# Softmax and memory heads: the value product of a block issued two steps behind its transpose instead of one, with three buffers for the split block

## What is computed

```python
sc = jnp.einsum('bhqd,bhkd->bhqk', q_blk, k).astype(jnp.float32) * scale
sc = jnp.where(key_pos <= q_pos, sc, -jnp.inf)
p = jax.nn.softmax(sc, axis=-1)
return jnp.einsum('bhqk,bhkd->bhqd', p.astype(v.dtype), v)
```

## Time and profile before

| | |
|---|---|
| median of 3 runs | 3078.08 us (3076.92 to 3081.86) |
| span of the profiled execution | 3078.6 us |
| its own time apart from the span | not recorded; the span stands for it |
| mean granted TensorE clock | 0.939 of 2.4 GHz |
| latent heads, five loop passes and the closing one | 1840 to 2261 us of the span |
| memory heads' attention | 113 to 157 us and 1567 to 1611 us |

### The profile page before, as it was taken

The page is one execution under the profiler, slowest core; times in us unless marked ns, Lnnn a source line. Parts: engine busy times, 40 slices in busy tenths (PEclk is TensorE's granted clock), DMA queues, the critical chain, the costliest instruction groups (busy, mean ns, idle before and its releaser), DMA issues. The chain is left out here.

```text
span 3078.6 us, 40579 instructions
## 1 busy us (share of the span) xinstructions
PE 2705.0 (88%) x13104; PEld 2209.8 (72%) x13104; DVE 1480.0 (48%) x2547; ACT 1295.7 (42%) x2794; POOL 1038.7 (34%) x722
## 2 busy tenths in 40 slices
PE   5679999878999998998668668888879899998999
PEld 4567777657788887887548657777757688887887
DVE  5636666744755553111562236666643755553111
ACT  4436566634333332222442246666633433332222
POOL 2035555530544443443102011111120544443443
PEclk9899999989999999999788879999989999999999
DMA  3021000041222223454102000000041222223454
GB/s 111 11 65 28 28 27 27 7 171 69 82 82 82 82 82 144 143 171 147 39 14 57 23 12 18 19 18 18 9 169 69 82 82 82 82 82 134 143 171 140
DMA packets 143097, 232.38 MB, mean 75 GB/s; under 512 B 17056, under 2 KB 93856, under 8 KB 143008
## 3 DMA queue, kind: packets, MB, share of 16 engines
q1 hardware_dynamic: 143008, 231.24, 22.7%
HBM read 182.98 MB, written 48.23 MB: 75 GB/s over the span
## 5 line engine op out<-in xcount | busy, mean ns | idle before, releaser
L1487 POOL TENSOR_TENSOR l0s_run_lo<-l0s_run,l0s_run_hi 128x512 fp32r<-128x512 f32 (+3 forms) x144 | 177.2, 1231 | 200.9 <-DVE l0s_run_hi L1653 200.9
L365 POOL TENSOR_TENSOR l0f_dn_lo<-l0f_dn_raw,l0f_dn_hi 128x1024 fp32r<-128x1024 f32 x44 | 106.0, 2411 | 138.9 <-ACT l0f_dn_hi L431 138.9
L365 POOL TENSOR_TENSOR l1f_dn_lo<-l1f_dn_raw,l1f_dn_hi 128x1024 fp32r<-128x1024 f32 x44 | 106.0, 2412 | 138.3 <-ACT l1f_dn_hi L431 138.3
L82 PE MATMUL banks<-l0f_dn_hi,l0f_a_hi 128*128 128x512 f32 x352 | 139.4, 396 | 8.9 <-issue 5.3
L82 PE MATMUL banks<-l1f_dn_hi,l1f_a_hi 128*128 128x512 f32 x352 | 138.6, 394 | 9.5 <-issue 5.3
L82 PE MATMUL banks<-l1f_T_hi,l1f_op_hi 128*128 128x512 f32 x352 | 139.3, 396 | 7.4 <-DVE l1f_T_lo L538 7.2
L82 PE MATMUL banks<-l0f_T_hi,l0f_op_hi 128*128 128x512 f32 x352 | 140.1, 398 | 6.1 <-DVE l0f_T_lo L538 5.9
L84 PE MATMUL banks<-l0f_T_hi,l0f_op_lo 128*128 128x512 f32 x352 | 139.0, 395 | 0.0
L83 PE MATMUL banks<-l0f_dn_lo,l0f_a_hi 128*128 128x512 f32 x352 | 138.9, 395 | 0.0
L84 PE MATMUL banks<-l0f_dn_hi,l0f_a_lo 128*128 128x512 f32 x352 | 138.8, 394 | 0.0
L84 PE MATMUL banks<-l1f_T_hi,l1f_op_lo 128*128 128x512 f32 x352 | 138.8, 394 | 0.0
(11 more groups left out here) (480 smaller groups left out, 8572.1 us busy)
## 6 DMA issues: line engine op xcount, KB each, us to landing
l0f_raw<-in_w_ffn_gu_dram SPq DMA_DIRECT2D x22, 1024.0 KB, 5.2
l0f_dn_raw<-in_w_ffn_down_dram SPq DMA_DIRECT2D x44, 512.0 KB, 3.9
l1f_raw<-in_w_ffn_gu_dram SPq DMA_DIRECT2D x22, 1024.0 KB, 5.1
l1f_dn_raw<-in_w_ffn_down_dram SPq DMA_DIRECT2D x44, 512.0 KB, 3.9
hidden_rows<-l0f_hid SPq DMA_DIRECT2D x22, 512.0 KB, 2.7
l0f_a_raw<-hidden_rows SPq DMA_DIRECT2D x44, 256.0 KB, 3.1
hidden_rows<-l1f_hid SPq DMA_DIRECT2D x22, 512.0 KB, 2.7
l1f_a_raw<-hidden_rows SPq DMA_DIRECT2D x44, 256.0 KB, 3.0
```

The costliest lines, as they stand in the source:

```text
L82: pe.matmul(out, l_hi, r_hi, start=first, stop=False, skip_group_check=True)
L365: pool.tensor_tensor(dn_lo[e][:], dn_raw[e][:], as_f32(dn_hi[e][:]), ALU.subtract).then_inc(dn_lo_done, 1)
L1487: pool.tensor_tensor(run_lo[t % NR][:, f:HALF], run[t % NR][:, f:HALF], as_f32(run_hi[t % NR][:, f:HALF]), ALU.subtract).then_inc(run_spli ...
```

## The change

V is issued behind T(tau) for block tau-2 instead of tau-1 (`LAG`), and `pt_hi` and `pt_lo` have three buffers instead of two (`NP`); there are still two PSUM banks for the transposes. The end of a job, E, moves with V by one step. "values 0", which overwrites the values of head 0, moves from tau 13 to 14, since V(11) still reads them. The third buffer needs room: some small tiles move between two memory areas, and `k_rope` is placed where the latent heads' tiles may overlap it.

```diff
+    NP = 3
+    LAG = 2
...
-        self.pt_hi = [mem(f"{tag}_pt_hi{s}", [P, HALF], F32R) for s in range(2)]
-        self.pt_lo = [mem(f"{tag}_pt_lo{s}", [P, HALF], F32R) for s in range(2)]
-        self.nmx, self.rsum, self.rinv = (mem(f"{tag}_{n}", [P, 4]) for n in ("nmx", "rsum", "rinv"))
+        self.pt_hi = [mem(f"{tag}_pt_hi{s}", [P, HALF], F32R) for s in range(self.NP)]
+        self.pt_lo = [(low_mem if s == 2 else mem)(f"{tag}_pt_lo{s}", [P, HALF], F32R) for s in range(self.NP)]
+        self.nmx, self.rsum, self.rinv = (low_mem(f"{tag}_{n}", [P, 4]) for n in ("nmx", "rsum", "rinv"))
...
-                if tau:
-                    steps.append(("V",) + self.of(tau - 1))
-                    if j == 0:
+                if tau >= self.LAG:
+                    steps.append(("V",) + self.of(tau - self.LAG))
+                    if n and j == self.LAG - 1:
                         steps.append(("E", n - 1))
...
-        steps += [("V",) + self.of(self.nt - 1), ("E", self.nj - 1)]
+        steps += [("V",) + self.of(tau) for tau in range(self.nt - self.LAG, self.nt)]
+        steps.append(("E", self.nj - 1))
...
-                act.wait_ge(self.pv_made, 1 + turn * self.nt + max(tau - 1, 0))
-                act.activation(self.pt_hi[tau % 2][:, c0:HALF], self.t_ps[tau % 2][:, c0:HALF],
+                act.wait_ge(self.pv_made, 1 + turn * self.nt + max(tau - self.NP + 1, 0))
+                act.activation(self.pt_hi[tau % self.NP][:, c0:HALF], self.t_ps[tau % 2][:, c0:HALF],
...
-              10: ["rotate 1", "turn 0"], 11: ["used 1", "turn 1"], 12: ["turn 2"], 13: ["values 0", "turn 3"],
-              14: ["turn 4"], 16: ["turn 5"], 18: ["turn 6"], 21: ["turn 7"]}
+              10: ["rotate 1", "turn 0"], 11: ["used 1", "turn 1"], 12: ["turn 2"], 13: ["turn 3"],
+              14: ["values 0", "turn 4"], 16: ["turn 5"], 18: ["turn 6"], 21: ["turn 7"]}
```

More of the change, by code:

```diff
@@ L771, with __init__ @@
 class Attend:
-    def __init__(self, nc, ctx, tag, mem, psum, k, jobs, keys_of, blocks_of, causal, scores, values, store,
+    NP = 3
+    LAG = 2
+    def __init__(self, nc, ctx, tag, mem, low_mem, psum, k, jobs, keys_of, blocks_of, causal, scores, values, store,
                  rows_mem, ring, score_banks, out_banks=(6, 7), plan=None, extras={}):
@@ L893, in pe @@
                     pe.wait_ge(self.out_done, 1 + turn * self.nj + max(n + 1 - len(self.o_ps), 0))
-                pe.matmul(o[:, c0:HALF], self.values(h, j), self.pt_hi[tau % 2][:, c0:HALF],
+                pe.matmul(o[:, c0:HALF], self.values(h, j), self.pt_hi[tau % self.NP][:, c0:HALF],
                           start=j == 0, stop=False, skip_group_check=True)
-                pe.matmul(o[:, c0:HALF], self.values(h, j), self.pt_lo[tau % 2][:, c0:HALF], start=False,
+                pe.matmul(o[:, c0:HALF], self.values(h, j), self.pt_lo[tau % self.NP][:, c0:HALF], start=False,
                           stop=tau + 1 == self.first[n + 1], skip_group_check=True).then_inc(self.pv_made, 1)
@@ L950, in dve @@
                 dve.wait_ge(self.hi_done, turn * self.nt + tau + 1)
-                dve.tensor_tensor(self.pt_lo[tau % 2][:, c0:HALF], self.t_ps[tau % 2][:, c0:HALF],
-                                  as_f32(self.pt_hi[tau % 2][:, c0:HALF]), ALU.subtract).then_inc(self.split_done, 1)
+                dve.tensor_tensor(self.pt_lo[tau % self.NP][:, c0:HALF], self.t_ps[tau % 2][:, c0:HALF],
+                                  as_f32(self.pt_hi[tau % self.NP][:, c0:HALF]), ALU.subtract).then_inc(self.split_done, 1)
             elif kind == "E":
@@ L1330, in memory_heads @@
         jobs = [(h, half) for h in range(MEM_HEADS) for half in range(2)]
-        at = Attend(nc, ctx, f"{tag}a", mem, psum, k, jobs, lambda tile: MEM, lambda half: MEM // P, False, scores,
+        at = Attend(nc, ctx, f"{tag}a", mem, mem, psum, k, jobs, lambda tile: MEM, lambda half: MEM // P, False, scores,
                     lambda h, j: v[:, j, h, :],
@@ L2067, in scores @@
             return pe.matmul(out[:, rows], k["ident_r"][:], k["causal"][:], start=False, stop=True, skip_group_check=True)
-        at_ = Attend(nc, ctx, f"{tag}a", low, psum, k, [(h, half) for h in range(2) for half in range(2)],
+        at_ = Attend(nc, ctx, f"{tag}a", low, mem, psum, k, [(h, half) for h in range(2) for half in range(2)],
                      lambda tile: (tile + 1) * P, lambda half: 4 * half + 4, True, scores,
@@ L2360, in build @@
                 ckv = {h: mem(f"ckv_{h}", [P, KV_RANK // P, S], F32R) for h in ("hi", "lo")}
-                k_rope, k_rot = mem("k_rope", [P, NS, ROPE]), mem("k_rot", [P, NS, ROPE])
+                k_rot = mem("k_rot", [P, NS, ROPE])
                 tab = [mem(f"rope_tab{n}", [P, NS, ROPE // 2]) for n in range(4)]
                 k_ss = mem("k_ss", [P, NS])
+                heads_at = mem.at
+                k_rope = mem("k_rope", [P, NS, ROPE])
                 latent_inputs(nc, f"{tag}i", k, w_in[:, 0:q_mem_at], a["mla_q_norm"][0], a["mla_kv_norm"][0],
@@ L2367, in build @@
                 latent_heads(nc, f"{tag}a", k, a["mla_w_q_up"][0], a["mla_w_kv_up"][0], a["mla_g_qn"][0],
-                             a["mla_g_kn"][0], cq, ckv, tab, k_rot, k_ss, mem.at, psum, ot_dram)
+                             a["mla_g_kn"][0], cq, ckv, tab, k_rot, k_ss, heads_at, psum, ot_dram)
             project_and_swiglu(nc, f"{tag}f", k, x, x_dram, x_att, a_dram, ot_dram, a["w_out"][layer], a["ln_ffn"][layer],
```

## The result

The changed kernel took 3089.83 us in the median of 18 runs (3083.7 to 3095.1), the one before 3081.05 us in as many on the same chip (3073.45 to 3087.26). The ratio is 1.0029, with a 95% interval of 1.0022 to 1.0035: some 9 us slower, outside the range of the prediction. The kernel before now lies 3.0 us above its median of the time of the prediction, so that the difference alone, put on the 3078.08 us of then, would end at 3086.9, at the edge of that range. The profiled execution has a span of 3091.4 us against 3078.6. The two profiled executions are 12.8 us apart, the medians 8.8: the figures of the traces are of one execution each and make the loss look somewhat larger than it is.

What follows compares the result with a forecast made beforehand. No engine is full; a ring of transpose, split and multiply sets the loop pass. +3.0 - 3.5 - 0.6 = -1.1 us on the 3078.6 us span gives 3077.5, and 3077.0 us as median; 8-in-10 range 3068 to 3087 us.

Steps and rivals of the forecast that it cites:

- signs of being wrong: New profile: a loop pass under 74 us, no new `o_out` wait, or granted clock clearly above 0.93 or below 0.88.
- rival 1: Whole kernel: V's 44.0 us of waits vanish and nothing takes their place, 3034 us; chance 0.04.
- "values 0" from step 13 to 14: Loop pass: the moved copy stands ten steps ahead of its reader in the next pass, so costs 0.
- Tau 16 to 18: Loop pass: split comes 0.6 us earlier, output V(16) needs 0.6 us behind it; 0 us, bound +0.4.
- Tau 6: Loop pass: V(4) waits for the single output bank, emptied one step later; +0.6 us.
- Tau 9 to 11: Loop pass: turn 1 at most 0.4 us earlier, slow first turn 0.44 us; 0 us, bounds -0.4 and +1.5.
- gap before turn 1: Loop passes: TensorE idles about 5 us, turns 1 to 3 run at 1.2 GHz; 3086 us, chance 0.18.
- Tau 20 to 23: Loop pass: score 21 goes ahead of V(19), VectorE gains its 0.47 us idle; -0.5 us, bounds 0 and -0.81.
- Tau 1: Loop pass: project 1 still waits for bank 7, and V(0) moves among back-to-back work at tau 2; +0.5 us.
- Loop passes: Five latent-head passes with projections: +0.6 us a pass, +3.0 us over five.
- Closing pass: Last latent-head pass, without projections: T goes before V, so blocks come faster; -3.5 us, bounds -2 and -6.
- Memory heads: Only the last block gains, some 0.3 us in each layer; -0.6 us, bounds 0 and -2.

Runs made afterwards that it cites:

- e8: Order of the kernel before (V one behind everywhere) with three buffers, "values 0" at tau 14 instead of 13: 3086.8 us, ratio 1.0017 to before.
- e3: Changed kernel, but in loop passes each job's last V is issued behind the next job's first T: 3073.3 us, ratio 0.9977 to before.
- e4: e3 with "values 0" back at tau 13 and a wait for V(11): 3070.3 us, ratio 0.9967 to before.
- e7: Changed kernel with six idle products in front of V(16) in each loop pass: 3083.0 us, ratio 1.0007 to before.
- e5: Changed kernel, but in loop passes only V(15) is issued early, behind T(16): 3076.4 us, ratio 0.9984 to before.
- e6: Changed kernel, but in loop passes only V(3) is issued early, behind T(4): 3082.3 us, ratio 0.9998 to before.
- e1: Kernel before with V two behind only in the closing pass, plus third buffer and moved tiles: 3076.3 us, ratio 0.9988 to before.
- e12: e4 with early job ends in the closing pass too and eight idle products before turn 1: 3065.9 us, ratio 0.9934 to before.
- e10: e4 with V one behind in the memory heads: 3071.5 us, ratio 0.9977 to before.
- e9: e4 with fourteen idle products before turn 1 in each loop pass: 3066.3 us, ratio 0.9959 to before.

## Why the prediction was wrong

The time lay above the range, and of the prediction's own signs of being wrong one showed: a granted clock of 0.85 in one loop pass. Passes of 76.4 to 80.9 us lay above its 75 to 76.5.

**The waits: right.** V's waits for `pt_lo` gone, T, turn 1, project 1 and V(4), V(16) waiting in their place, turn 1 for 5.2 us: all as foretold. That the edit moves waits rather than removes them was the right reading, and rival 1 (3034 us) was rightly given little.

**"values 0" from step 13 to 14: 0.** This step failed. I asked who waits for the values, and not beside whom GpSimd works. VectorE's scaling of the 1024-key row went from 0.75 to 1.83 us, and T(16) waited for it. e8 prices this at +5 to 6 us in the order of before; with early ends, from e3 to e4, it was 2.9 us by the medians and 3.5 by the traces, and in the changed kernel the five passes lost 3.6 us from turn 4 to T(16). So the step cost some 3 to 6 us. That the same subtraction of GpSimd took anything from 1.48 to 2.01 us in the kernel before stood in its trace, and would have told that something beside it matters.

**Tau 16 to 18: 0 (bound +0.4).** This failed too, but not in the wait. What stands behind T(18) came at 64.70 us of the pass (V(16), 1985.25) and at 62.92 before (V(17), 1979.87), +1.78, of which T(16) had brought 1.64 along: the wait's end was costed rightly. What was missed is what runs behind it. One idle piece of 2.08 us stood where 1.15 had stood; behind it the clock fell in four of five passes, and 19 matmuls took 1.6 us longer in three of them and 2.6 in one. I had reckoned with the clock at turn 1 only. e7 (-6.8 us, the stretch back at 1.00 in every pass) shows this cause and its size; e5 (-13.5 us) shows the place, but holds a gain over before as well.

**Tau 6: +0.6.** The term was nearly right, +0.8 at project 6, of which 0.3 is left by turn 1. What it lacked is again the clock: in one of the passes project 6 went at 0.61, 1.6 us more. e6 recovers 7.5 us, more than the term's 3.0; most of the rest came behind V(16), which e6 leaves as it is.

**Tau 9 to 11: 0 (-0.4 and +0.4).** Near. Turn 1 came 0.3 us later where project 6 had lost 0.8, so the order gave back 0.5. From turn 1 to turn 4 the five passes took 41.7 us, against 38.8 before; but e1 and e8, whose loop passes have the order of before, took 39.5 and 41.9, so how much of these 3.0 us the longer gap brought is not shown. That slow turns cost time e12 shows, and that the old order had them too the prediction had said. The rival "gap before turn 1" gave a total near the measured one (3086 us), but put +1.5 to +2 us a pass on this place, which has at most 0.6 of the 3.1 us lost a pass. No run fills this gap in the changed kernel itself.

**Tau 20 to 23: -0.5.** From turn 6 to the next T(0) the second pass took 10.76 us before and 10.86 after: no gain, with slow T and V at its start in it. Tau 1's +0.5 did not show: project 1 stood at 5.65 and 5.71, T(4) +0.2.

**Loop passes +3.0**: measured +15.3. **Closing pass -3.5**: measured -3.6, and e1 gave -4.2 us in the median. **Memory heads -0.6**: from the first to the last `pt_lo` 40.4 us in each layer, before 40.2 and 40.3; no gain, and e10 can't resolve it.

So the sum missed by two steps, each put at nothing: a neighbour on another engine (3 to 6 us), and the clock behind a wait whose end had been costed rightly (6.8 us). The two with the terms as they stood make more than the 8.8 us measured; the figures come from different kernels and don't add exactly. The Trainium skill, SBUF — State Buffer, section Who interferes with whom, says that a VectorE `tensor_scalar` in a two-port mode and GpSimd exclude each other for a whole instruction, and that issue order decides who blocks. No row here names the mode in which the scaling ran; the trace agrees on the size: VectorE's 1.83 is 0.75 and 1.08 of GpSimd's 1.28, and GpSimd's 1.94 before is the 1.28 of the new trace and VectorE's 0.67. On who blocks it isn't so plain, since in the second case GpSimd had started 0.13 us earlier and was the one prolonged.

## What to carry to other kernels

When a step moves, write down what each engine runs beside it at the new place, GpSimd against VectorE above all, and not only who waits for it: here a moved copy cost some 3 to 6 us by its neighbour. When two waits become one, or a wait grows past what stood there before, give the matmuls behind it a price at the lower clock as well: here it fell in four of five passes behind 2.08 us, and in none behind 1.15. And when a product is issued later, keep what empties its bank where it was: moving only the last product of each job back turned +0.29% into -0.23%.

## What the runs showed that I had not expected

- Idle products can pay: six of them, 1.63 us of useless work, shortened the kernel by 6.8 us; TensorE had a granted clock of 1.00 in the stretch behind, where it had 0.63 in three passes and 0.50 in one.
- The same wait brings the clock down in some passes and not in others: behind V(4)'s 1.29 us, project 6 took 2.82 us in one pass and 4.43 two passes later, in one execution; behind V(16)'s 2.08 us the clock fell in four of five passes of the changed kernel and in two of five of e6.
- Equal work ran at either level of the clock, or partly at each, from pass to pass: the fourteen equal products of e9 took 6.15, 5.00 and 3.49 us in three successive passes (1958.80, 2033.01 and 2106.04).
- A meeting of GpSimd's subtraction and VectorE's scaling costs one or the other most or all of the length of the other's instruction (1.28 and 0.67 us): 1.83 us in place of 0.75, or 1.94 in place of 1.28.
